# A DeltaNet scan with values scaled on GpSimd, decayed keys on ScalarE, another product order, and the gate's input split inside the scan

## The chip, the cores and the metric

The kernel runs on one core of one Trainium2 chip. The metric is the device time of one execution in microseconds (us), as a median of runs. It is one program with five engines that work through instruction lists of their own and wait for each other by semaphores: TensorE (PE, with its weight loads PEld), VectorE (DVE), ScalarE (ACT), GpSimd (POOL) and SyncE (SP), which issues the weight transfers.

## What is computed

Two blocks of a transformer on 256 latent and 256 context tokens of width 1024, in float32. The change touches only the second block, from the gated delta rule to the gate:

```python
def gated_delta_chunked(q, k, v, beta, g, s0):
    ...
    a = jnp.where(strict, jnp.einsum("bhnid,bhnjd->bhnij", kb, k) * decay, 0.0)
    t_inv = lax.linalg.triangular_solve(a + eye, ...)
    u = t_inv @ (v * beta[..., None])
    w = t_inv @ (kb * jnp.exp(g)[..., None])
    kd = k * jnp.exp(g_last[..., None] - g)[..., None]
    def step(s, inp):
        v_new = u_i - jnp.einsum("bhcd,bhde->bhce", w_i, s)
        o_i = (jnp.einsum("bhcd,bhde->bhce", qg_i, s)
               + jnp.einsum("bhij,bhje->bhie", attn_i, v_new))
        s = s * jnp.exp(gl_i)[..., None, None] + jnp.einsum("bhcd,bhce->bhde", kd_i, v_new)
        return s, o_i
...
gates = jax.nn.sigmoid((h @ w_gate + b_gate).astype(jnp.float32))   # 1024 -> 3072
```

It runs in two directions, over 4 chunks of 128 tokens (the kernel's own size) and 4 heads of 128.

## The kernel before

**Inverse by levels.** `level_step` (L1013) builds the inverse of four chunk matrices in 24 steps (`STEPS`), two groups of products a step. VectorE masks the first product (L2082), subtracts the second from `Y` (L2086) and masks the transposed root for the next level (L2071). GpSimd makes `YR` (L2275). The last four steps finish `Y` for chunks 0, 1, 2, 3 in that order.

**Scan.** `TT[d]` is `Y` under the triangular mask of direction d: eight masks (L2093), all on VectorE, after the last level step. Then come four steps s. `SCAN` gives the chunk of each: 2, 3, 0, 1 for direction 0 and 3, 2, 1, 0 for direction 1. Chunks 0 and 1 are the latent ones, so only steps 2 and 3 have an output. At each step and for both directions:

- VectorE scales the values by beta (L2108, into `Xb` at step 0 and `BV` after) and the keys by their decay (L2115, `KD`), in four instructions of 128x128 for the four heads;
- TensorE multiplies keys by the state (group `ks`) and queries by the state (`o1`), and VectorE makes X from `ks` and `BV` (L2123);
- TensorE makes the new values `vn` = `TT` times X, and ScalarE copies them out (L1256, called in the loop of L1505);
- TensorE makes the state's addition `S` from `KD` and `vn`, and the second half of the output, `o2`. VectorE updates the state (L2145, L2147) and adds both halves to the output (L2134, L2154).

A group is one PSUM bank. `heads` (L995) fills it with four products, at L998 as the profile shows them; a float32 product leaves two records in it. Groups take banks 0 to 4 in turn. After each of the first three steps stands one block of the conditioning matrix (`ada_block`, L607, 16 records), which also frees a slot of the three-slot weight ring, so that SyncE can issue a transfer of the gate's weights.

**Between scan and gate.** TensorE folds the conditioning (L618) and transposes the output (L1087). VectorE adds the bias (L1576) and copies the transposes out (L2162). The gate's input h is split in two parts so that products run in a faster number format: ScalarE rounds it to `gate_hi` (L1516) and VectorE takes the rest, `gate_lo` (L2165), in eight pieces. The weights are split the same way in parts of 128x1024, with room for three: `w_hi` by ScalarE (L1271), `w_lo` by VectorE (L1732). A part has 8 x 3 products (L550, L551, L552) and makes one of 24 gate groups. With `lead=True` the first three parts run interleaved. `keep_busy` (L480) issues filler products whose result is thrown away: 12 before the first `vn`, 14 and 2 at the gate (two records each).

## Time and profile before

| | us |
|---|---|
| median of three runs | 1786.26 |
| lowest, highest | 1779.35, 1787.01 |
| span of the profiled execution | 1778.1 |
| levels of the inverse | some 1318 to 1372 |
| scan, first `vn` to the transposes | 1378 to 1417 |
| first product of the gate | 1423.37 |

The page gives a span for the profiled execution, from its first to its last instruction, and no time of its own beside it; the times of the runs lie 1.3 to 8.9 us above it. All times of the rows are us from the start of that span. A row of the timeline merges neighbouring instructions of one kind: start, how long they last together, engine, line, count, and in brackets how long the engine was idle before and what ended that.

### The profile page before, as it was taken

Reading aid. Unit: us, or ns where it says so; the run is one execution under the profiler, and the core shown is the slowest. Engines: PE = TensorE matmul, PEld = TensorE weight load, DVE = VectorE, ACT = ScalarE, POOL = GpSimd, SP = SyncE. Lnnn points to the kernel's source line nnn. Section 1 sums busy time; section 2 is a strip of 40 time slices with the busy share of each in tenths; the row PEclk is TensorE's granted clock in tenths of the full one; section 3 lists DMA queues with packets and bytes.
Section 4 is the critical chain, followed back from the end, with each engine's and each line's share of the span. In section 5 each row is a group of like instructions: output and inputs, shape, how many; then the busy total and the mean of one; then the engine's idle time right before and its main releaser. Section 6 shows DMA issues by size and latency. Waiting matters only on the chain.

```text
span 1778.1 us, 26580 instructions
## 1 busy us (share of the span) xinstructions
PE 1704.4 (96%) x10450; PEld 1364.7 (77%) x10450; DVE 969.5 (55%) x1732; ACT 692.9 (39%) x1255; POOL 193.1 (11%) x210
## 2 busy tenths in 40 slices
PE   5999999999999999999999999899999999999997
PEld 2775457778888887454689999777689799989997
DVE  3454654643434344346736666775588855555454
ACT  3433564332323232234635444643310266344443
POOL 1012442100000001043000000100134000200000
PEclk9999999999999999999999999999999999999999
DMA  9225981222222224334043555133130334435342
GB/s 407 84 95 239 378 331 48 95 95 95 95 95 95 95 95 151 130 143 189 2 179 150 190 190 188 53 145 139 53 137 2 142 143 153 178 143 190 148 158 74
DMA packets 21323, 254.02 MB, mean 143 GB/s; under 512 B 2256, under 2 KB 4560, under 8 KB 5584
## 3 DMA queue, kind: packets, MB, share of 16 engines
q1 hardware_dynamic: 18144, 242.51, 35.5%
q10 hardware_dynamic: 3056, 9.82, 1.5%
q8 instruction: 84, 1.38, 0.3%
q14 instruction: 39, 0.32, 0.1%
HBM read 251.26 MB, written 1.05 MB: 142 GB/s over the span
## 4 chain that ended last, share of the span: by engine, by line
PE 83%; DVE 8%; ACT 4%; issue 2%; DMA 2%; POOL 1%; DVEq 0%; POOLq 0%; ACTq 0%; SPq 0%
PE bank L550 18%; PE bank L551 17%; PE bank L552 17%; PE bank L507 10%; PE bank L998 4%; PE bank L607 3%; PE bank L686 3%; PE bank L712 2%; DVE w_lo L1732 2%; PE bank L694 2%; DMA weights<-in_ada 2%; ACT w_hi L1271 1%; DVE root L1593 1%; PE bank L661 1%; POOL root L2229 1%
## 5 line engine op out<-in xcount | busy, mean ns | idle before, releaser
L1732 DVE TENSOR_TENSOR w_lo<-weights,w_hi 128x1024 fp32r<-128x1024 f32 (+2 forms) x286 | 331.9, 1169 | 109.0 <-ACT w_hi L1271 106.2
L1271 ACT ACTIVATE w_hi<-weights 128x1024 fp32r<-128x1024 f32 (+2 forms) x286 | 287.7, 1013 | 231.8 <-PE bank L552 227.4
L550 PE MATMUL bank<-h_hi,w_hi 128*128 128x256 f32 (+1 forms) x1024 | 338.8, 331 | 14.2 <-DVE w_lo L1732 7.9
L552 PE MATMUL bank<-h_hi,w_lo 128*128 128x256 f32 (+1 forms) x1024 | 335.1, 327 | 0.0
L551 PE MATMUL bank<-h_lo,w_hi 128*128 128x256 f32 (+1 forms) x960 | 311.0, 324 | 0.0
L550 PEld LDWEIGHTS bank<-h_hi,w_hi 128*128 128x128 f32 x1024 | 192.6, 188 | 41.2 <-issue 19.6
L552 PEld LDWEIGHTS bank<-h_hi,w_lo 128*128 128x128 f32 x1024 | 192.2, 188 | 19.0
L551 PEld LDWEIGHTS bank<-h_lo,w_hi 128*128 128x128 f32 x960 | 180.8, 188 | 15.2
L551 PE MATMUL bank<-mlp_hidden_lo,w_hi 128*128 128x512 f32 (+1 forms) x512 | 174.4, 341 | 0.0
L550 PE MATMUL bank<-mlp_hidden_hi,w_hi 128*128 128x512 f32 (+1 forms) x512 | 173.2, 338 | 0.6 <-DVE w_lo L1732 0.6
L552 PE MATMUL bank<-mlp_hidden_hi,w_lo 128*128 128x512 f32 (+1 forms) x512 | 172.7, 337 | 0.0
L507 PE MATMUL bank<-slab,weights 128*128 128x256 f32 (+2 forms) x656 | 163.6, 402 | 0.9 <-ACT slab L1210 0.2
L507 PEld LDWEIGHTS bank<-slab,weights 128*128 128x128 f32 (+1 forms) x656 | 120.6, 186 | 42.3 <-issue 19.7
L2229 POOL TENSOR_TENSOR root<-root,sq 128x512 f32<-128x512 f32 (+1 forms) x42 | 47.7, 1136 | 940.5 <-ACT sq L1197 937.6
L1794 DVE SCALAR_TENSOR_TENSOR x<-bank,mod,x 128x256 f32<-128x256 f32 x104 | 47.4, 481 | 171.1 <-PE bank L552 171.1
L550 PEld LDWEIGHTS bank<-mlp_hidden_hi,w_hi 128*128 128x128 f32 x512 | 96.5, 189 | 13.8 <-issue 1.1
L1780 DVE TENSOR_TENSOR slab<-bank,slab 128x512 f32<-128x512 f32 (+1 forms) x64 | 35.7, 558 | 130.3 <-ACT slab L1301 130.3
L552 PEld LDWEIGHTS bank<-mlp_hidden_hi,w_lo 128*128 128x128 f32 x512 | 96.1, 188 | 11.5
L551 PEld LDWEIGHTS bank<-mlp_hidden_lo,w_hi 128*128 128x128 f32 x512 | 96.1, 188 | 11.0
L1301 ACT ACTIVATE slab<-bank 128x512 f32<-128x512 f32 (+1 forms) x64 | 31.4, 490 | 153.9 <-PE bank L552 153.9
L998 PE MATMUL bank<-slab 128*128 128x128 f32 x656 | 81.1, 277 | 7.8 <-DVEq L2128 3.4
L607 PE MATMUL bank<-weights,cond 128*32 128x512 f32 x576 | 71.8, 617 | 17.1 <-DMA weights<-in_ada 17.1
(276 smaller groups left out, 2849.0 us busy)
## 6 DMA issues: line engine op xcount, KB each, us to landing
weights<-in_ada SPq DMA_DIRECT2D x36, 2048.0 KB, 9.6
weights<-in_mlp_up SPq DMA_DIRECT2D x16, 2048.0 KB, 8.2
weights<-in_mlp_down SPq DMA_DIRECT2D x16, 2048.0 KB, 8.2
weights<-in_ffn_in SPq DMA_DIRECT2D x11, 2048.0 KB, 7.9
weights<-in_in SPq DMA_DIRECT2D x8, 2048.0 KB, 8.0
weights<-in_gate SPq DMA_DIRECT2D x6, 2048.0 KB, 7.9
weights<-in_ffn_out SPq DMA_DIRECT2D x8, 1408.0 KB, 6.1
weights<-in_even_in SPq DMA_DIRECT2D x3, 2048.0 KB, 12.5
```

Of the source, the lines that this page charges most:

```text
L507: last = mm(b[rows, 0:width], lhsT(k), rhs(k), start=k == 0, stop=k == kc - 1)
L550: mm(b[:, 0:width], wh, hi(k), start=k == 0, stop=False)
L551: mm(b[:, 0:width], wh, lo(k), start=False, stop=False)
L552: return mm(b[:, 0:width], wl, hi(k), start=False, stop=k == kc - 1)
L607: ins = mm(banks[ADA_BANK][strip, :], cond[:, n // 2, k, window], w[:, k, :], start=at == 0 and k < 4, stop=at == ADA_SIZES[batch] - 1 and ...
L686: close(mm(b[:, 0:u["n"]], u["q"], u["k"], start=True, stop=True), t)
L998: ins = mm(b[:, hd * P:(hd + 1) * P], lhsT(hd), rhs(hd), start=True, stop=True)
L1271: A(split_part(w_hi, q), raw_part(q), ACT.Copy).then_inc(sem("w_hi_ready"), 1)
L1732: V.tensor_tensor(split_part(w_lo, q), raw_part(q), split_part(w_hi, q).bitcast(F32), ALU.subtract)\
L1780: V.tensor_tensor(relu[name][:, i % 3, 0:width], bank(tb)[:, 0:width], relu[name][:, i % 3, 0:width], ALU.mult).then_inc(free(tb), 1)
L1794: ins = V.scalar_tensor_tensor(out=x[:, i % 8, cols], in0=bank(t)[:, cols], scalar=mod[n][:, 40 + i % 8, s:s + 1], in1=x[:, i % 8, cols], ...
L2229: nc.gpsimd.tensor_tensor(sq_sum[:, 0:width], sq_sum[:, 0:width], sq[:, c % 2, 0:width], ALU.add)\
```

## The change

Four things are done:

1. Of the eight masks VectorE keeps two, those of step 0 (`TT[0]` chunk 2, `TT[1]` chunk 3), each right behind the subtraction that finishes its `Y`. GpSimd makes the other six, a pair for each later step.
2. GpSimd scales the values: for step 0 before the levels, into `VN` (whose place in `work` changes), for the later steps into `Xb`, where X is then formed in place. ScalarE scales the keys. It does step 0's during the last level step, the others after the state product before.
3. TensorE does both `ks` first, then for each direction `o1` and at once `vn`. The filler of the scan and of the gate is gone.
4. ScalarE rounds the gate's input after step 2's new values, and the first weight parts are split during step 3 and behind it. The gate's products follow the scan directly and part by part, not interleaved. The transposes of the output come after the third part, the fold after the fourth; VectorE's copies and bias follow.

The semaphores of the norms are joined in two (`norm_sq`, `norm_added`), with counts in place of names.

```diff
@@ -332,7 +332,7 @@
...
-        Xb, VN, KD, BV, S = ([work[:, (2 * n + d) * 512:(2 * n + d + 1) * 512] for d in range(2)] for n in range(5))
+        Xb, S, KD, VN = ([work[:, (n + d) * 512:(n + d + 1) * 512] for d in range(2)] for n in (0, 2, 4, 7))
...
+                def state_read(tag, d, rows):
+                    t = SCAN[d][s]
+                    heads((tag, d, s), lambda hd: rows[:, hd, t * P:(t + 1) * P], lambda hd: S[d][:, hs(hd)])
+
+                def new_values(d):
+                    t = SCAN[d][s]
+                    if s:
+                        pe.wait_ge(sem("X_ready"), 2 * (s - 1) + d + 1)
+                        pe.wait_ge(sem("TT_rest"), 2 * (s - 1) + d + 1)
+                    else:
+                        pe.wait_ge(sem("X0_ready"), d + 1)
+                        pe.wait_ge(sem("TT_ready"), d + 1)
+                    heads(("vn", d, s), lambda hd: TT[d][:, t, hs(hd)], lambda hd: (Xb if s else VN)[d][:, hs(hd)])
+
+                if s:
+                    for d in range(2):
+                        drained(pe, ("S", d, s - 1))
+                        state_read("ks", d, kT)
+                for d in range(2):
+                    if SCAN[d][s] < 2:
+                        state_read("o1", d, qT)
+                    new_values(d)
...
-                    n = 2 * s + d
-                    if s:
-                        drained(pe, ("S", d, s - 1))
-                        heads(("ks", d, s), lambda hd: kT[:, hd, t * P:(t + 1) * P], lambda hd: S[d][:, hs(hd)])
-                    if t < 2:
-                        heads(("o1", d, s), lambda hd: qT[:, hd, t * P:(t + 1) * P], lambda hd: S[d][:, hs(hd)])
-                for d in range(2):
-                    t = SCAN[d][s]
-                    n = 2 * s + d
-                    if n:
-                        pe.wait_ge(sem("X_ready"), n + 1)
-                    else:
-                        b = open_group(("vn", d, s))
-                        keep_busy(b, 12)
-                        pe.wait_ge(sem("TT_ready"), 8)
-                        pe.wait_ge(sem("X_ready"), n + 1)
-                    heads(("vn", d, s), lambda hd: TT[d][:, t, hs(hd)], lambda hd: Xb[d][:, hs(hd)], opened=n == 0)
...
-            ada_fold(4)
-            for t in range(2):
-                pe.wait_ge(sem("o_ready"), t + 1)
-                b = open_group(("oT", t))
-                for hd in range(DN_HEADS):
-                    ins = nc.tensor.transpose(b[:, hs(hd)], otok[:, t, hs(hd)], ident)
-                close(ins, ("oT", t))
+
+            def output_turned():
+                for t in range(2):
+                    pe.wait_ge(sem("o_ready"), t + 1)
+                    b = open_group(("oT", t))
+                    for hd in range(DN_HEADS):
+                        ins = nc.tensor.transpose(b[:, hs(hd)], otok[:, t, hs(hd)], ident)
+                    close(ins, ("oT", t))
+
             def gate_steps(m):
+                if m == 2:
+                    output_turned()
+                if m == 3:
+                    ada_fold(4)
...
             split_linear("gate", range(6), lambda k: gate_hi[:, k, :], lambda k: gate_lo[:, k, :], LAT,
                          lambda m: ("gate", m), lambda k, m: pe.wait_ge(sem("gate_in"), k + 1) if m == 0 else None,
-                         lead=True, after=gate_steps, idle=(14, 2))
+                         after=gate_steps)
...
                 copy_out(("kt", t), ktok[:, t, :])
+            def decayed_keys(d, s):
+
+                t = SCAN[d][s]
+                drained(act, ("kt", t))
+                if s:
+                    filled(act, ("S", d, s - 1))
+                for hd in range(DN_HEADS):
+                    ins = A(KD[d][:, hd * P:(hd + 1) * P], ktok[:, t, hd * P:(hd + 1) * P], ACT.Copy,
+                            scale=eKD[:, t, 4 * d + hd:4 * d + hd + 1])
+                ins.then_inc(sem("KD_ready"), 1)
+
+            act.wait_ge(sem("G_exp"), 3)
+            filled(act, ("u", STEPS - 1))
+            for d in range(2):
+                decayed_keys(d, 0)
+            gate_first = parts_before("in2")
             for s in range(4):
+                if s == 3:
+                    filled(act, ("S", 1, 2))
+                    split_until(gate_first + 1)
                 for d in range(2):
                     if s:
                         filled(act, ("o2" if SCAN[d][s - 1] < 2 else "S", d, s - 1))
                     else:
-                        act.wait_ge(sem("TT_ready"), 8)
                         filled(act, ("tt", STEPS - 1))
                     copy_out(("vn", d, s), VN[d])
+                if s < 2:
+                    for d in range(2):
+                        decayed_keys(d, s + 1)
...
+            filled(act, ("vn", 1, 3))
+            split_until(gate_first + PARTS)
             ada_copy(4)
-            filled(act, ("oT", 1))
...
+                    t, d = (n - 1) % 4, (n - 1) % 4 - 2
+                    if n > STEPS - 4 and d >= 0:
+                        drained(dve, ("tt", n - 1))
+                        V.tensor_tensor(by_head(TT[d][:, t, :]), by_head(Y[:, t, :]), spread(k2(f"until{d}")), ALU.mult)\
+                            .then_inc(sem("TT_ready"), 1)
...
-            for t in range(4):
-                drained(dve, ("tt", STEPS - 4 + t))
-                for d in range(2):
-                    V.tensor_tensor(by_head(TT[d][:, t, :]), by_head(Y[:, t, :]), spread(k2(f"until{d}")), ALU.mult)\
-                        .then_inc(sem("TT_ready"), 1)
+            def rest_of_gate(c):
+                dve.wait_ge(sem("gate_in_hi"), c + 1)
+                V.tensor_tensor(gate_lo[:, c, :], h[:, c, 0:LAT], gate_hi[:, c, :].bitcast(F32), ALU.subtract)\
+                    .then_inc(sem("gate_in"), 1)
+
...
-                    dst = Xb[d] if s == 0 else BV[d]
-                    for hd in range(DN_HEADS):
-                        ins = V.tensor_scalar(dst[:, hs(hd)], vtok[t][:, hd // 2, (hd % 2) * P:(hd % 2 + 1) * P],
-                                              col(beta, hd), None, ALU.mult)
-                    link(ins)
-                    if s == 0:
-                        V.engine_nop().then_inc(sem("X_ready"), 1)
-                    if s < 3:
-                        for hd in range(DN_HEADS):
-                            ins = V.tensor_scalar(KD[d][:, hs(hd)], ktok[:, t, hs(hd)], col(eKD, hd), None, ALU.mult)
-                        link(ins)
-                        V.engine_nop().then_inc(sem("KD_ready"), 1)
...
                         filled(dve, ("ks", d, s))
+                        dve.wait_ge(sem("BV_ready"), 2 * (s - 1) + d + 1)
                         for hd in range(DN_HEADS):
                             ins = V.scalar_tensor_tensor(out=Xb[d][:, hs(hd)], in0=bank(("ks", d, s))[:, hs(hd)],
-                                                         scalar=col(nbeG, hd), in1=BV[d][:, hs(hd)],
+                                                         scalar=col(nbeG, d, hd), in1=Xb[d][:, hs(hd)],
...
+                    if s == 3:
+                        split_until(split[0] + 1)
...
+                if s == 3:
+                    filled(dve, ("vn", 1, 3))
+                    for c in range(DC):
+                        rest_of_gate(c)
+                    filled(dve, ("o2", 1, 3))
+                    split_until(split[0] + 1)
...
-            ada_bias(4)
-            for t in range(2):
-                filled(dve, ("oT", t))
...
             for i in range(24):
                 split_until(PART_END[("gate", i)] + PARTS - 1)
+                if i == 3:
+                    for t in range(2):
+                        filled(dve, ("oT", t))
+                        V.tensor_copy(onT[:, :, t * P:(t + 1) * P], by_head(bank(("oT", t))[:, :]))\
+                            .then_inc(free(("oT", t)), 1)
+                if i == 4:
+                    ada_bias(4)
...
+            def scaled_values(dst, d, t, name):
+
+                for a in range(2):
+                    ins = nc.gpsimd.tensor_tensor(
+                        by_head(dst)[:, 2 * a:2 * a + 2, :], vtok[t][:, a, :].rearrange("p (h c) -> p h c", c=P),
+                        beta[:, t, 4 * d + 2 * a:4 * d + 2 * a + 2].unsqueeze(2).to_broadcast([P, 2, P]), ALU.mult)
+                ins.then_inc(sem(name), 1)
+
+            filled(pool, ("f1", 3))
+            pool.wait_ge(sem("gate_parts"), 3)
+            for d in range(2):
+                drained(pool, ("vt", SCAN[d][0]))
+                scaled_values(VN[d], d, SCAN[d][0], "X0_ready")
...
+            filled(pool, ("tt", STEPS - 3))
+            for s in range(1, 4):
+                for d in range(2):
+                    drained(pool, ("vt", SCAN[d][s]))
+                    if s > 1:
+                        filled(pool, ("vn", d, s - 1))
+                    scaled_values(Xb[d], d, SCAN[d][s], "BV_ready")
+                for d in range(2):
+                    t = SCAN[d][s]
+                    drained(pool, ("tt", STEPS - 4 + t))
+                    nc.gpsimd.tensor_tensor(by_head(TT[d][:, t, :]), by_head(Y[:, t, :]),
+                                            k2(f"until{d}").unsqueeze(1).to_broadcast([P, DN_HEADS, P]), ALU.mult)\
+                        .then_inc(sem("TT_rest"), 1)
```

VectorE, from the last level steps to the first state copy. L2082 and L2086 (now L2122 and L2126) belong to the levels, L2093 (L2131) is the mask, L2108 values, L2115 keys, L2145 (L2180) the state's copy; ISA rows only signal. Before:

```order
L2082 TENSOR_TENSOR slab<-bank,consts 128x512
L2086 TENSOR_TENSOR slab<-slab,bank 128x512 x2
L2093 TENSOR_TENSOR slab<-slab,consts 128x512 x8
L2108 TENSOR_SCALAR slab<-slab 128x128 x4
L2112 ISA
L2115 TENSOR_SCALAR slab<-slab 128x128 x4
L2117 ISA
```

Now:

```order
L2122 TENSOR_TENSOR slab<-bank,consts 128x512
L2126 TENSOR_TENSOR slab<-slab,bank 128x512
L2131 TENSOR_TENSOR slab<-slab,consts 128x512
L2126 TENSOR_TENSOR slab<-slab,bank 128x512
L2131 TENSOR_TENSOR slab<-slab,consts 128x512
L2180 COPY slab<-bank 128x128 x4
```

Two masks remain, one of them between the last two subtractions, and the scaled sets are gone.

TensorE, from the last level steps over the scan to the gate. L998 (now L1006) are the groups of `heads`, L483 the filler, L607 (L615) conditioning, L618 the fold, L1087 the transposes. Before:

```order
L998 MATMUL bank<-slab 128x128 x20
L483 MATMUL bank<-shared 128x256 x12
L998 MATMUL bank<-slab 128x128 x16
L607 MATMUL bank<-weights,cond 32x512 x8
L998 MATMUL bank<-slab 128x128 x24
L607 MATMUL bank<-weights,cond 32x512 x8
L998 MATMUL bank<-slab 128x128 x40
L607 MATMUL bank<-weights,cond 32x512 x8
L998 MATMUL bank<-slab 128x128 x32
L618 MATMUL bank<-shared,root 128x32 x4
L1087 MATMUL bank<-shared,slab 128x128 x8
L483 MATMUL bank<-shared 128x256 x14
```

Now:

```order
L1006 MATMUL bank<-slab 128x128 x36
L615 MATMUL bank<-weights,cond 32x512 x8
L1006 MATMUL bank<-slab 128x128 x24
L615 MATMUL bank<-weights,cond 32x512 x8
L1006 MATMUL bank<-slab 128x128 x40
L615 MATMUL bank<-weights,cond 32x512 x8
L1006 MATMUL bank<-slab 128x128 x32
L558 MATMUL bank<-gate_hi,w_hi 128x256
```

The same groups stand there (20 + 16 = 36), without the filler, and the gate's first product follows the scan's last one.

GpSimd, from the diagonal matrices ahead of the levels (L2263, now L2297) to the sums at the gate's end (L2280, now L2340). L2275 (L2322) is `YR`, L2304 half a set of scaled values, L2334 a mask. Before:

```order
L2263 TENSOR_TENSOR slab<-shared,slab 128x512 x8
L2275 TENSOR_TENSOR slab<-slab,consts 128x512 x24
L2280 TENSOR_TENSOR slab<-slab 128x256 x8
```

Now:

```order
L2297 TENSOR_TENSOR slab<-shared,slab 128x512 x8
L2304 TENSOR_TENSOR slab<-slab 128x256 x4
L2322 TENSOR_TENSOR slab<-slab,consts 128x512 x24
L2304 TENSOR_TENSOR slab<-slab 128x256 x4
L2334 TENSOR_TENSOR slab<-slab,consts 128x512 x2
L2304 TENSOR_TENSOR slab<-slab 128x256 x4
L2334 TENSOR_TENSOR slab<-slab,consts 128x512 x2
L2304 TENSOR_TENSOR slab<-slab 128x256 x4
L2334 TENSOR_TENSOR slab<-slab,consts 128x512 x2
L2340 TENSOR_TENSOR slab<-slab 128x256 x8
```

Sixteen halves and six masks came to GpSimd, in the order in which the steps use them.

## Rows read from the trace of the kernel before

**Rows 1.** The page: the span, and the busy time of TensorE.
```profile
span 1778.1 us, 26580 instructions
PE 1704.4 (96%) x10450; PEld 1364.7 (77%) x10450; DVE 969.5 (55%) x1732; ACT 692.9 (39%) x1255; POOL 193.1 (11%) x210
```

**Rows 2.** Windows: length, busy PE, PEld, DVE, ACT, POOL, granted clock, DMA share, GB/s.
```profile
1385.00:1396.00 11.00, 8.60 (x69) 6.62 (x70) 8.12 (x33) 1.19 (x2) 0.00 (x0) 1.00 0.52 192
...
1436.00:1560.00 124.00, 122.24 (x906) 117.22 (x905) 71.12 (x100) 64.59 (x94) 12.07 (x13) 1.00 0.44 168
```

**Rows 3.** Timeline of TensorE, scan and gate: start, length, line, count, idle time before.
```profile
1378.22 1.13 PE L998 MATMUL bank<-slab 128*128 128x128 f32 x8 [1.35 <-DVEq L2112]
...
1383.05 1.92 PE L607 MATMUL bank<-weights,cond 128*32 128x512 f32 x16
...
1389.34 4.23 PE L998 MATMUL bank<-slab 128*128 128x128 f32 x32 [2.38 <-DVEq L2128]
1393.50 1.92 PE L607 MATMUL bank<-weights,cond 128*32 128x512 f32 x16
...
1406.33 1.93 PE L607 MATMUL bank<-weights,cond 128*32 128x512 f32 x16
1408.19 7.53 PE L998 MATMUL bank<-slab 128*128 128x128 f32 x64
...
1417.51 6.21 PE L483 MATMUL bank<-shared 128*128 128x256 f32 x28
1423.37 0.47 PE L550 MATMUL bank<-gate_hi,w_hi 128*128 128x256 f32 x1
...
1434.46 0.36 PE L550 MATMUL bank<-gate_hi,w_hi 128*128 128x256 f32 x1 [0.55 <-ACT w_hi L1271]
...
1437.42 0.28 PE L550 MATMUL bank<-gate_hi,w_hi 128*128 128x256 f32 x1
```

**Rows 4.** Timeline of VectorE, the same stretch.
```profile
1371.72 0.69 DVE L2086 TENSOR_TENSOR slab<-slab,bank 128x512 f32<-128x512 f32 x1 [0.38 <-PE bank L998]
1372.33 4.90 DVE L2093 TENSOR_TENSOR slab<-slab,consts 128x512 f32<-128x512 f32 x8
...
1388.08 2.29 DVE L2123 SCALAR_TENSOR_TENSOR slab<-bank,slab 128x128 f32<-128x128 f32 x8
...
1418.54 2.77 DVE L2165 TENSOR_TENSOR gate_lo<-slab,gate_hi 128x256 fp32r<-128x256 f32 x8
1421.25 3.50 DVE L1732 TENSOR_TENSOR w_lo<-weights,w_hi 128x1024 fp32r<-128x1024 f32 x3
```

**Rows 5.** Timeline of ScalarE: four scaled 128x128 pieces, and a copy of new values.
```profile
1266.28 1.28 ACT L1492 ACTIVATE slab<-slab 128x128 f32<-128x128 f32 x4 [1.33 <-DVEq L2017]
...
1379.46 0.60 ACT L1256 ACTIVATE slab<-bank 128x512 f32<-128x512 f32 x1 [68.31 <-PE bank L998]
```

**Rows 6.** Groups of GpSimd by line and shape: count, busy us, mean ns.
```profile
L2275 POOL TENSOR_TENSOR slab<-slab,consts 128x512 f32<-128x512 f32 x24 | 30.5, 1270 | 39.2 <-DVE slab L2086 19.7 <-DVE slab L2065 17.2 <-PE bank L998 2.3
L2238 POOL TENSOR_TENSOR slab<-slab,stat 128x256 f32<-128x256 f32 x32 | 20.7, 647 | 42.0 <-DVE stat L1704 41.9
```

**Rows 7.** DMA issues of the gate's weights: KB each, median us to landing.
```profile
weights<-in_gate SPq DMA_DIRECT2D x6, 2048.0 KB, 7.9
```

**Rows 8.** Timelines of VectorE and GpSimd where both work, ahead of and in the levels.
```profile
1311.98 0.69 DVE L2065 TENSOR_TENSOR slab<-slab,shared 128x512 f32<-128x512 f32 x1
...
1313.30 1.26 DVE L2065 TENSOR_TENSOR slab<-slab,shared 128x512 f32<-128x512 f32 x1
...
1327.23 0.68 DVE L2071 TENSOR_TENSOR slab<-bank,consts 128x512 f32<-128x512 f32 x1
...
1312.75 1.27 POOL L2275 TENSOR_TENSOR slab<-slab,consts 128x512 f32<-128x512 f32 x1 [15.96 <-DVE slab L2065]
...
1327.39 1.27 POOL L2275 TENSOR_TENSOR slab<-slab,consts 128x512 f32<-128x512 f32 x1 [0.95 <-DVE slab L2086]
```

**Rows 9.** Windows after TensorE's last product, columns as in rows 2.
```profile
1771.00:1773.00 2.00, 0.00 (x0) 0.00 (x0) 1.97 (x5) 0.00 (x0) 0.00 (x0) 0.54 0.01 3
```

68 lines of the change are left out of this document (30 added, 38 removed).

## The prediction, written before the run

> **What bounds the kernel now.** I read the page first: TensorE is busy for 96% of the span [rows 1], so only a place where it waits, or works for nothing, can give time back. Next I read the busy time by stretch. The gate's products are TensorE's own: 122.24 of 124 us busy, all at a granted clock of 1.00 [rows 2]. The scan before them is not: TensorE is busy for 8.60 of 11 us between 1385 and 1396. So I read the scan engine by engine in order of time. TensorE's rows [rows 3] show a wait of 1.35 us before the first new-value product (1378.22), one of 2.38 us before that of step 1 (1389.34), and at 1417.51 a run of 28 filler records, 6.21 us of products on a constant that nobody reads (`keep_busy`), until the gate's first product at 1423.37. More such filler (24 records) stands ahead of 1378.22. VectorE's rows [rows 4] say what is waited for. From 1372.33 it applies eight masks, at 4.90/8 = 0.61 us each; then it scales values (L2108) and keys, four instructions of 128x128 a set, at every step; the 1.35 us end with the mark behind the first values (L2112) [rows 3]. Both stand in front of what TensorE needs next. After the scan come eight rests of the gate's input (2.77 us) and three rests of weights (3.50 us), all after the transposes of the output.
>
> **The units of the sum.** One product group (four heads) has 8 records. The 64 records from 1408.19 take 7.53 us; without the last one's tail, some 0.15 us, that is 0.92 us a group. The stretches with waits look like 0.95, and I take 0.95. From its start to the next start a conditioning block (16 records, L607) holds TensorE for 1.85 us (1.92 less the tail) [rows 3]. One part of the gate's weights is 24 products; from 1434.46 to 1437.42 that is 2.96 with a slow first one, 2.88 without (24 x 0.12). ScalarE copies new values in 0.60 us [rows 5]. For a hand-over between engines I take 0.13 us: the copy starts at 1379.46, 1.24 us after its product of 1.1 us.
>
> **Part 1, the masks (gain 6.0 us).** Before, the first new-value product starts at 1378.22, behind eight masks and the first values. Now VectorE applies one mask right behind the subtraction it belongs to. The subtraction before the last ends near 1371.4, since the last one starts at 1371.72 after an idle 0.38 us [rows 4]. So the first mask runs 1371.4 to 1372.1 and TensorE starts at 1372.2. This pushes the last subtraction from 1371.72 to 1372.1; it and the second mask end near 1373.5. The first values are ready long before, from GpSimd at about 1297. The last piece of the order above shows the six masks on GpSimd. A mask of that form costs it 1.27 us, and half a set of values I put at the nearest row, 0.65 us [rows 6], so a pair of sets is 2.6 and a pair of masks 2.5 us. They start at 1368.9 and are due at steps 1, 2 and 3. For step 2 GpSimd begins when the step 1 products are done (about 1382.2) and is finished by 1387.3, while TensorE wants the two masks from 1389.8. For step 3 it is finished by 1396.7 and wanted at 1401.1. The spare is at least 2.5 us, so I cost them at nothing; the cover is the state products, the conditioning block and the read-outs.
>
> **Part 2, steps 0 to 2 (gain 0.5 + 2.0 + 1.5 us).** First product to first conditioning block is 4.83 us before (1378.22 to 1383.05). Now the second product waits for the second mask (1.4 us after the first); with its copy and the two state products I get 4.4, say 0.5 less. From that block to the next is 10.45 us before (1383.05 to 1393.50). Now it is 1.85 + 6 x 0.95 = 7.55, plus 0.9 for X: VectorE's correction takes 1.14 us a set (2.29 for two at 1388.08 [rows 4]) and can't hide wholly behind one group. That makes 8.45, or 2.0 less. From there to the third block it is 12.83 us before (1393.50 to 1406.33) and now 1.85 + 10 x 0.95 = 11.35. The read-outs stand ahead of each new-value product and hide the correction, so 1.5 less. The decayed keys cost ScalarE 1.28 us a set by the nearest row [rows 5]; two sets (2.5 us) follow each state product, 5 us before TensorE wants them, in time in which ScalarE does nothing now.
>
> **Part 3, end of scan to the gate (gain 7.5 us).** Before, 1406.33 to 1423.37 is 17.04 us. Now TensorE has 1.85 + 8 x 0.95 = 9.45 us of work and then the gate's first product, with no fold, no transposes and no filler between. What must be ready then: one part of weights split on both engines (w_hi near 1397, w_lo 1402.7) and the first rest of the gate's input, which VectorE writes after two corrections, one w_lo and two read-outs, by my count at 1405.8. TensorE finishes at 1405.9. That is a near tie, so I add 0.1: 9.55, or 7.5 less. The rests then come every 0.35 us (2.77/8), and TensorE uses one in 0.36. The gate's first block has landed: its transfer is issued when the first conditioning block has used its slot, and takes 7.9 us [rows 7]; now that is near 1378.6, and the block is there by 1387. The next ones come behind blocks two and three, wanted at 1412 and 1424.
>
> **Part 4, the first gate parts (gain 0).** First to fourth part is 11.09 us before (1423.37 to 1434.46), with filler and a wait in it. Now three parts of 2.88, 0.6 us in which the second part's w_lo is late (VectorE comes to it only after eight rests), and 0.9 for the two transposes, moved here, make 10.1. The fold, another 0.95 (0.98 before the scan's end), moved behind the fourth part, makes 11.05. From there the stretch is TensorE's, as before. Copying the transposed output and the bias moved with them, into VectorE time that has room (71 of 124 us busy [rows 2]).
>
> **The sum.** 6.0 + 0.5 + 2.0 + 1.5 + 7.5 + 0 = 17.5 us less. The page's execution has a span of 1778.1 us [rows 1], which becomes 1760.6; the three times are 1.3, 8.2 and 8.9 us above that span. On the median it gives 1786.3 - 17.5 = 1768.8 us. With no wait in the scan at all (28 groups and 3 blocks, 32.15 us, against some 33.7 in my count) and none at the second part, the gain would be 19.7 us. With every near tie lost, 14 us.
>
> **A page against the trace: one lock for two engines.** The trace shows VectorE held by GpSimd in one kind of instruction: L2065, two inputs in SBUF, takes 0.69 us alone (1311.98), but 1.26 us when GpSimd's instruction of 1312.75 to 1314.02 is under way (1313.30) [rows 8]. L2071, which reads a bank and one SBUF tensor, keeps its 0.68 us (1327.23) beside a GpSimd instruction from 1327.39 on. The Trainium skill, page SBUF — State Buffer, section SBUF: two separate sides, says just this: the pair is an exclusive lock, kept for a whole instruction, against two-SBUF-input VectorE instructions. By that rule, moving work to GpSimd is a danger in itself. In the scan, however, nearly all of VectorE's work reads a bank. What is exposed is the two masks. The second is released together with GpSimd's first mask, by the same subtraction; if GpSimd takes the lock first, the second product comes up to 1.3 us later. At 1311.98 and 1312.75 VectorE went first (0.04 us against 0.08 after the release), so I leave it out of the sum and keep it for rival (a). By the skill's rule with GpSimd first the sum would be 16.2 us and the time 1770.1; with VectorE first it stands.
>
> **Rivals.**
> (a) *Ties lost.* The second mask is blocked (1.3 us), hand-overs cost 0.2 rather than 0.13 us (0.7), and gate_lo and the second part come 1 to 2 us later. The gain is then 9 to 14 us, 1772 to 1777. For it: three near ties. Against: each has a row.
> (b) *The gate gives it back.* Parts 1 to 3 are now split while VectorE also adds the last read-outs and copies the output. If the split ran a part late (2.9 us) for three parts, 8.7 us would be lost: gain 8.8, 1777.5. Against: a part costs VectorE 1.2 us of 2.88.
> (c) *GpSimd sets the scan.* From 2.5 us over, each further microsecond goes on the path. It needs masks and values at twice their rows, 10.2 us for 5.1: 2 x 2.6 us late, gain 12, 1774.
> (d) *Slower: the clock.* The filler keeps TensorE working; 28 products of it (56 records) go. After its last product at the end TensorE's granted clock falls to 0.54 within 1771 to 1773, that is toward 1.2 GHz [rows 9]. If that came at the scan's start and stayed, 32.15 us of work would take twice as long: 1786.3 - 17.5 + 32.2 = 1801. It decides from 17.5 us of work at 1.2 GHz. Against: TensorE works for 32.15 of 33.7 us in the new scan, more than in 1385 to 1396, where waits of up to 2.38 us left the clock at 1.00 [rows 2, 3].
> (e) *The change doesn't do what it says.* The new order excludes that: the masks, the filler and the scaled sets have left their places.
>
> **How the numbers follow.** Forecast (14 to 19.7 us less): 0.68. (a) 0.15. (b) and (c) together 0.10. (d) 0.04. 0.03 for a gain near zero by a cause I don't see. Predicted: 1768.8 us. The range takes the gain from 10.5 to 19.7 us and the spread of the times themselves (1779.4 to 1787.0): 1758 to 1776. A difference of over 0.5% (8.9 us) is about what a measurement of this kernel tells from none. Faster by that: all of the forecast, (a), and part of (b) and (c), 0.87. Within: 0.09. Slower: 0.04.
>
> **What would show it.** In the changed trace: the first new-value product 0.8 us behind the first mask; conditioning blocks 8.5 and 11.4 us apart (10.45 and 12.83 now); the gate's first product 9.5 us after the third block starts, with the gate_lo row touching it; six GpSimd masks of 1.3 us; a granted clock of 1.00 throughout. Wrong would be: the second mask at 1.2 us or more, TensorE waiting for GpSimd, or waits between the first gate parts above 1 us.

## The result, and the profile after

The changed kernel takes 1765.28 us (median of four runs, 1762.58 to 1766.02), the kernel before beside it 1784.9 us. The ratio is 0.9895 with a 95% interval of 0.988 to 0.991: 1.05% faster. In a second comparison it was 0.9889 (0.9871 to 0.9906).

The page after, beside [rows 1]: the span is 14.7 us shorter, TensorE's busy time 10.1 us.

```profile
span 1763.4 us, 26446 instructions
PE 1694.3 (96%) x10394; PEld 1356.3 (77%) x10394; DVE 953.5 (54%) x1670; ACT 700.5 (40%) x1279; POOL 210.4 (12%) x232
```

Windows of the changed kernel over scan and gate, columns as in [rows 2]. TensorE is busy for 29.25 of the 30 us from 1380 to 1410, where [rows 2] showed 8.60 of 11, and the granted clock stays at 1.00.

```profile
1380.00:1390.00 10.00, 9.51 (x80) 6.35 (x75) 5.35 (x20) 5.09 (x16) 4.46 (x6) 1.00 0.56 211
1390.00:1400.00 10.00, 10.00 (x92) 9.30 (x92) 7.55 (x26) 4.60 (x12) 5.21 (x7) 1.00 0.56 211
1400.00:1410.00 10.00, 9.74 (x88) 8.42 (x77) 7.73 (x23) 3.62 (x6) 0.00 (x0) 1.00 0.56 210
1410.00:1425.00 15.00, 14.62 (x123) 14.44 (x123) 11.06 (x15) 6.93 (x9) 0.00 (x0) 1.00 0.37 142
```

TensorE's timeline of the changed kernel, to be held against [rows 3]. L1006 are the groups of `heads`, L615 conditioning, L558 a gate product, L1098 the transposes, L626 the fold.

```profile
1375.57 1.13 PE L1006 MATMUL bank<-slab 128*128 128x128 f32 x8 [0.49 <-issue]
1376.90 3.03 PE L1006 MATMUL bank<-slab 128*128 128x128 f32 x24 [0.20 <-issue]
1379.86 1.93 PE L615 MATMUL bank<-weights,cond 128*32 128x512 f32 x16
...
1384.17 4.30 PE L1006 MATMUL bank<-slab 128*128 128x128 f32 x32 [0.40 <-DVEq L2155]
1388.41 1.92 PE L615 MATMUL bank<-weights,cond 128*32 128x512 f32 x16
1390.26 9.20 PE L1006 MATMUL bank<-slab 128*128 128x128 f32 x80
1399.39 1.92 PE L615 MATMUL bank<-weights,cond 128*32 128x512 f32 x16
1401.24 7.53 PE L1006 MATMUL bank<-slab 128*128 128x128 f32 x64
1409.04 0.36 PE L558 MATMUL bank<-gate_hi,w_hi 128*128 128x256 f32 x1 [0.26 <-DVE gate_lo L2137]
...
1412.52 0.36 PE L558 MATMUL bank<-gate_hi,w_hi 128*128 128x256 f32 x1 [0.38 <-DVE w_lo L1772]
...
1418.35 1.03 PE L1098 MATMUL bank<-shared,slab 128*128 128x128 f32 x8
1419.14 0.36 PE L558 MATMUL bank<-gate_hi,w_hi 128*128 128x256 f32 x1
1422.10 0.97 PE L626 MATMUL bank<-shared,root 128*128 128x32 f32 x8
1422.90 0.36 PE L558 MATMUL bank<-gate_hi,w_hi 128*128 128x256 f32 x1
```

No wait is above 0.49 us, and no filler stands between. Two rows run on without a gap: 80 records from 1390.26, 64 from 1401.24.

VectorE's timeline beside it, to be held against [rows 4]: L2126 is a level's subtraction, L2131 a mask, L2180 the state's copy, L2150 X, L1772 a rest of weights, L2163 the first half of the output, L2137 the rests of the gate's input.

```profile
1374.06 0.69 DVE L2126 TENSOR_TENSOR slab<-slab,bank 128x512 f32<-128x512 f32 x1 [0.20 <-PE bank L1006]
1374.78 0.69 DVE L2131 TENSOR_TENSOR slab<-slab,consts 128x512 f32<-128x512 f32 x1
1375.39 0.68 DVE L2126 TENSOR_TENSOR slab<-slab,bank 128x512 f32<-128x512 f32 x1
1376.11 0.69 DVE L2131 TENSOR_TENSOR slab<-slab,consts 128x512 f32<-128x512 f32 x1
1378.96 1.90 DVE L2180 COPY slab<-bank 128x128 f32<-128x128 f32 x8 [2.16 <-PE bank L1006]
...
1402.44 2.37 DVE L2150 SCALAR_TENSOR_TENSOR slab<-bank,slab 128x128 f32<-128x128 f32 x8 [1.89 <-PE bank L1006]
1404.92 1.23 DVE L1772 TENSOR_TENSOR w_lo<-weights,w_hi 128x1024 fp32r<-128x1024 f32 x1
1406.07 2.28 DVE L2163 SCALAR_TENSOR_TENSOR slab<-bank,slab 128x128 f32<-128x128 f32 x8
1408.46 2.77 DVE L2137 TENSOR_TENSOR gate_lo<-slab,gate_hi 128x256 fp32r<-128x256 f32 x8
```

**A measure that the rest of the kernel doesn't blur.** I cut every span in three: the *arrival*, up to the start of VectorE's last-but-one subtraction; the *landmark*, from there to the start of the gate's fifth part (1437.42 in [rows 3], 1422.90 after); and what follows. The arrival lies ahead of the scan. That subtraction in VectorE's timeline of the kernel before:

```profile
1370.66 0.69 DVE L2086 TENSOR_TENSOR slab<-slab,bank 128x512 f32<-128x512 f32 x1 [0.20 <-PE bank L998]
```

| kernel | median us | ratio (95%) | arrival | landmark | what follows |
|---|---|---|---|---|---|
| before | 1784.9 | | 1370.66 | 66.76 | 340.68 |
| after | 1765.28 | 0.9895 (0.988 to 0.991) | 1374.06 | 48.84 | 340.50 |
| after, again | 1764.77 | 0.9889 (0.9871 to 0.9906) | 1373.72 | 48.84 | 340.44 |
| e1 before, no filler | 1786.76 | 1.0011 (1.0002 to 1.002) | 1373.41 | 70.26 | 340.63 |
| e2 masks behind | 1762.87 | 0.9882 (0.9865 to 0.9898) | 1370.42 | 48.84 | 340.44 |
| e3 masks ahead | 1773.13 | 0.993 (0.991 to 0.9951) | 1375.21 | 56.04 | 340.55 |
| e4 sets on VectorE | 1772.49 | 0.994 (0.9921 to 0.9959) | 1372.48 | 57.34 | 340.48 |
| e5 gate late | 1770.39 | 0.9917 (0.9895 to 0.9939) | 1374.46 | 55.41 | 340.43 |
| e6 old order | 1764.6 | 0.9896 (0.9873 to 0.9918) | 1370.83 | 49.50 | 340.57 |
| e7 GpSimd busy | 1765.01, one run | | 1372.96 | 49.79 | 340.45 |
| e8 rest early | 1763.95 | 0.9884 (0.9867 to 0.99) | 1375.32 | 47.74 | 340.54 |
| e9 filler back | 1769.03 | 0.9914 (0.9899 to 0.9929) | 1373.21 | 52.86 | 340.53 |
| e10 both | 1763.4 | 0.9882 (0.9867 to 0.9898) | 1373.38 | 47.74 | 340.58 |

The last column is the same within 0.25 us in all thirteen. The whole effect sits in the landmark: 66.76 - 48.84 = 17.92 us. The arrival scatters over 4.9 us. In these two traces it is 3.40 us later in the changed kernel, which leaves 17.92 + 0.18 - 3.40 = 14.7 us between the spans. Most of that scatter is TensorE's clock, not the change. I took windows of 10 us up to 1370 and added up TensorE's busy time times what the granted clock lacks to 1.00. The loss is 2.9 us before and 6.0 after; it is 5.7 in e1, whose code up to there is that of before and whose arrival is 2.75 us later. Over all thirteen traces it runs from 1.7 (e2, the earliest arrival) to 6.2 us (e8, the latest), and a line through loss and arrival has a slope of 1.0, with every trace within some 0.8 us of it.

### The profile page after: what moved, and what is told of

It reads as the page before. It is cut to its first block, busy times and chain, and to the rows that moved or that the text cites. A ratio compares the mean times of both kernels' runs of the same rounds, so it can differ in the third digit from the quotient of the medians.

```text
span 1763.4 us, 26446 instructions
## 1 busy us (share of the span) xinstructions
PE 1694.3 (96%) x10394; PEld 1356.3 (77%) x10394; DVE 953.5 (54%) x1670; ACT 700.5 (40%) x1279; POOL 210.4 (12%) x232
## 3 DMA queue, kind: packets, MB, share of 16 engines
HBM read 251.26 MB, written 1.05 MB: 143 GB/s over the span
## 4 chain that ended last, share of the span: by engine, by line
PE 83%; DVE 7%; ACT 4%; issue 2%; DMA 2%; POOL 1%; DVEq 0%; POOLq 0%; ACTq 0%; SPq 0%
PE bank L558 18%; PE bank L560 17%; PE bank L559 17%; PE bank L515 11%; PE bank L1006 4%; PE bank L615 3%; PE bank L694 3%; PE bank L720 2%; DVE w_lo L1772 2%; PE bank L702 2%; DMA weights<-in_ada 2%; ACT w_hi L1287 1%; DVE root L1633 1%; PE bank L669 1%; POOL root L2263 1%
## 5 line engine op out<-in xcount | busy, mean ns | idle before, releaser
L1772 DVE TENSOR_TENSOR w_lo<-weights,w_hi 128x1024 fp32r<-128x1024 f32 (+2 forms) x286 | 331.9, 1169 | 103.4 <-ACT w_hi L1287 100.5
L558 PE MATMUL bank<-h_hi,w_hi 128*128 128x256 f32 (+1 forms) x1024 | 341.0, 333 | 14.2 <-DVE w_lo L1772 7.8
L558 PEld LDWEIGHTS bank<-h_hi,w_hi 128*128 128x128 f32 x1024 | 193.2, 189 | 40.1 <-issue 19.5
L558 PE MATMUL bank<-mlp_hidden_hi,w_hi 128*128 128x512 f32 (+1 forms) x512 | 174.9, 342 | 0.7 <-DVE w_lo L1772 0.7
L2263 POOL TENSOR_TENSOR root<-root,sq 128x512 f32<-128x512 f32 (+1 forms) x42 | 47.6, 1134 | 940.2 <-ACT sq L1213 937.4
L515 PEld LDWEIGHTS bank<-slab,weights 128*128 128x128 f32 (+1 forms) x656 | 120.6, 186 | 42.3 <-issue 19.7
L558 PEld LDWEIGHTS bank<-mlp_hidden_hi,w_hi 128*128 128x128 f32 x512 | 96.1, 188 | 12.4 <-issue 1.2
L615 PE MATMUL bank<-weights,cond 128*32 128x512 f32 x576 | 71.0, 611 | 17.5 <-DMA weights<-in_ada 17.5
L1341 ACT ACTIVATE slab<-bank,stat 128x512 f32<-128x512 f32 (+1 forms) x96 | 59.2, 617 | 62.9 <-DVE stat L1730 39.7
```

What stands on the lines that cost most here:

```text
L515: last = mm(b[rows, 0:width], lhsT(k), rhs(k), start=k == 0, stop=k == kc - 1)
L558: mm(b[:, 0:width], wh, hi(k), start=k == 0, stop=False)
L615: ins = mm(banks[ADA_BANK][strip, :], cond[:, n // 2, k, window], w[:, k, :], start=at == 0 and k < 4, stop=at == ADA_SIZES[batch] - 1 and ...
L1341: A(a["prob"][i % nprob][:, 0:u["n"]], bank(t)[:, 0:u["n"]], ACT.Exp, bias=stat[:, 1, i:i + 1], scale=a["scale"], accum_out=stat[:, 2, i:i ...
L1772: V.tensor_tensor(split_part(w_lo, q), raw_part(q), split_part(w_hi, q).bitcast(F32), ALU.subtract)\
L2263: nc.gpsimd.tensor_tensor(sq_sum[:, cols], sq_sum[:, cols], sq[:, c % 2, cols], ALU.add)\
```

## The experiments

**e1: is the filler dead weight?** The kernel before, without its filler products.

```diff
-                        keep_busy(b, 12)
...
-                         lead=True, after=gate_steps, idle=(14, 2))
+                         lead=True, after=gate_steps)
```

> The kernel before, with the filler of the scan (12 products) and of the gate (14 and 2) taken out and nothing else changed. Landmark: from the last level subtraction but one to the fifth gate part is 66.76 us before (1370.66 to 1437.42) and 48.84 us after the change (1374.06 to 1422.90). Theory A, the filler only fills waits for VectorE: 66 to 67 us, the first new-value product still 7.5 us after the landmark's start, granted clock 1.00 in the scan, time within 1 us of before. Theory B, the filler also holds the clock over TensorE's waits of some 6.5 us (before the first product) and 5 us (before the gate): the granted clock falls to 0.5 there, products at 1.2 GHz for some us, 3 to 10 us more than before.

TensorE's timeline and two windows of e1:

```profile
1380.97 6.29 PE L998 MATMUL bank<-slab 128*128 128x128 f32 x32 [6.53 <-DVEq L2111]
...
1426.89 0.55 PE L550 MATMUL bank<-gate_hi,w_hi 128*128 128x256 f32 x1 [5.05 <-DVE w_lo L1731]
...
1380.00:1390.00 10.00, 9.03 (x56) 7.44 (x57) 6.69 (x32) 1.19 (x2) 0.00 (x0) 0.70 0.01 2
...
1430.00:1440.00 10.00, 9.29 (x64) 9.09 (x62) 0.65 (x1) 2.10 (x4) 0.00 (x0) 0.81 0.00 0
```

The first product comes no sooner (7.56 us behind the subtraction, as before). Now TensorE stands idle for 6.53 us, and then works at a lower granted clock: the first four groups take 6.29 us. First product to first block is 6.22 us against 4.83. At the gate the wait is 5.05 us, the products run 0.21 us apart up to 1433.67 and 0.12 after, and first to fifth part is 16.78 us against 14.05. Only one thing comes back: third block to gate is 16.39 us against 17.04, so the gate's filler had outlasted its wait by 0.65 us. The landmark is 3.5 us longer, which is theory B at its lower end; the median time is 2.25 us longer, with an interval that just clears 1. The filler gained more where it stood than it cost.

**e9: and in the changed kernel?** The filler put back.

```diff
+                        if d == 0:
+                            keep_busy(open_group(("vn", d, s)), 12)
...
-                         after=gate_steps)
+                         after=gate_steps, idle=(14, 2))
```

> The changed kernel with TensorE's filler products put back: 12 ahead of the first new values, and 14 and 7 times 2 in the gate's first parts, as the kernel before has them. In the changed kernel TensorE waits 0.49 us ahead of the first new values and at most 0.4 us at any place in the gate's first parts. Theory A (the filler now has no wait to stand in, so it costs its own length): 12 products of 0.22 us minus 0.49 us is 2.2 us, and 28 products 6.2 us minus 0.6 us of waits is 5.6 us; landmark 48.84 + 7.8 = about 56.6 us, ratio about 0.993 to 0.994. Rival B (the filler is free, since it only stands while splits are awaited): landmark 49 to 50.

```profile
1374.08 5.34 PE L491 MATMUL bank<-shared 128*128 128x256 f32 x24
1379.26 2.96 PE L1006 MATMUL bank<-slab 128*128 128x128 f32 x24
```

My edit and my count were both partly wrong. `idle` acts only with `lead=True`, which the change gave up, so none stood at the gate. And a filler product leaves two records of 0.22 us, so twelve last 5.34 us. The first product then comes 6.05 us behind the subtraction instead of 1.51, and the landmark is 4.0 us longer. So theory A holds in kind, not in size: filler of 5.34 us without a wait of that length costs 4.0 us, and most of what comes off is the short waits of step 0, 0.49 us ahead of the first product and 0.51 us behind it. The filler at the gate was not tried.

**e3: all eight masks ahead again**, on VectorE, with the rest of the change kept.

```diff
-                        pe.wait_ge(sem("TT_ready"), d + 1)
+                        pe.wait_ge(sem("TT_ready"), 8)
...
+            for t in range(4):
+                drained(dve, ("tt", STEPS - 4 + t))
+                for d in range(2):
+                    V.tensor_tensor(by_head(TT[d][:, t, :]), by_head(Y[:, t, :]), spread(k2(f"until{d}")), ALU.mult)\
+                        .then_inc(sem("TT_ready"), 1)
...
```

> The changed kernel with all eight masks on VectorE behind the last subtraction and every new-value product waiting for all of them, as in the kernel before; everything else as changed. My sum: the first product comes 8 x 0.61 us and a hand-over behind the last subtraction, 6.4 us after the last but one in place of 1.51: landmark 53.6 us, 4.8 more than the changed kernel. Rival, part of that is given back because TensorE otherwise waits later in steps 0 and 1 (0.2 and 0.4 us): 53.0 us.

TensorE's timeline, and a window, of e3:

```profile
1381.88 6.40 PE L1006 MATMUL bank<-slab 128*128 128x128 f32 x32 [5.64 <-issue]
...
1380.00:1390.00 10.00, 8.12 (x48) 6.66 (x48) 3.55 (x11) 3.64 (x10) 0.00 (x0) 0.66 0.01 2
```

The first product is 5.16 us later, and after the 5.64 us of idleness four groups take 6.40 us: first product to first block is 6.34 us against 4.29. Together 7.2 us, of which the 2.05 behind the first product are the clock (0.66 in the window). My sum of 4.8 and the rival's 4.2 had no term for it; ahead of the first product my sum is near (5.16 us).

**e2: masks on VectorE, but behind.** The six masks of steps 1 to 3 on VectorE, after the two of step 0; GpSimd makes only the values.

```diff
+            for s in range(1, 4):
+                for d in range(2):
...
+                    V.tensor_tensor(by_head(TT[d][:, t, :]), by_head(Y[:, t, :]), spread(k2(f"until{d}")), ALU.mult)\
...
-                    nc.gpsimd.tensor_tensor(by_head(TT[d][:, t, :]), by_head(Y[:, t, :]),
...
```

> The changed kernel with the six later masks back on VectorE, directly behind the two of step 0; GpSimd keeps the values only. Theory A, only the two masks ahead of the first product matter, since VectorE waits 2.16 us for the first state product and TensorE has the conditioning block behind it: first state copy 1.5 us later, first product unchanged, landmark 48.8 to 49.8 us (48.84 in the changed kernel). Rival, moving the masks off VectorE is what gives the gain: 6 x 0.61 = 3.7 us on the path, landmark 52.5 us.

The landmark is 48.84 us, to the last digit that of the change. VectorE's six masks take 3.69 us; its first copy of the state comes 1.4 us later for them (6.27 us behind the last-but-one subtraction, not 4.90), and TensorE has the conditioning block to do meanwhile. What the masks gain is by which of them stand ahead of the first product, not by GpSimd.

**e4: the scaled sets on VectorE again**, steps 1 to 3.

```diff
...
+                        for hd in range(DN_HEADS):
+                            ins = V.tensor_scalar(Xb[d][:, hs(hd)], vtok[t][:, hd // 2, (hd % 2) * P:(hd % 2 + 1) * P],
+                                                  col(beta, d, hd), None, ALU.mult)
...
+                        if s < 3:
+                            for hd in range(DN_HEADS):
+                                ins = V.tensor_scalar(KD[d][:, hs(hd)], ktok[:, t, hs(hd)], col(eKD, d, hd), None, ALU.mult)
...
-                        dve.wait_ge(sem("BV_ready"), 2 * (s - 1) + d + 1)
```

> The changed kernel, but VectorE again makes the values times beta and the decayed keys of steps 1 to 3, ahead of each step's own values; the masks stay where the change puts them. Landmark: from the start of VectorE's last-but-one level subtraction to the start of the gate's fifth part, 48.84 us in the changed kernel, 66.76 in the kernel before. Theory A (the sets cost what VectorE spends between a state's last copy and the next product): each of steps 1 and 2 gets some 1.5 us longer, step 3, which has no keys, little; landmark 51.5 to 53, ratio to the kernel before about 0.991. Rival B (the sets fit into VectorE's idle time ahead of the step's own values): landmark 49 to 50, ratio as the changed kernel's, 0.989 to 0.990.

TensorE, VectorE and GpSimd in e4's timelines, and a window:

```profile
1386.97 6.16 PE L1006 MATMUL bank<-slab 128*128 128x128 f32 x32 [4.78 <-DVEq L2167]
...
1379.84 2.93 DVE L2151 TENSOR_SCALAR slab<-slab 128x128 f32<-128x128 f32 x4 [0.57 <-DVEq L2198]
...
1383.89 0.88 DVE L2151 TENSOR_SCALAR slab<-slab 128x128 f32<-128x128 f32 x4 [0.21 <-DVE slab L2156]
...
1374.63 7.85 POOL L2341 TENSOR_TENSOR slab<-slab,consts 128x512 f32<-128x512 f32 x6 [6.35 <-DVE slab L2123]
...
1387.00:1393.00 6.00, 6.00 (x32) 5.94 (x32) 1.73 (x7) 1.19 (x2) 0.00 (x0) 0.59 0.01 5
```

Both theories were too low: the landmark is 57.34 us, 8.5 more than after. Step 1 alone is 6.23 us longer (14.78 against 8.55). The scaled sets put 4.4 us of wait on the path (4.78 against 0.40): their own instructions, and 2.05 us in which VectorE's first four stand still beside GpSimd's masks (2.93 us where the next four take 0.88, until the last mask ends at 1382.48). The two fit together: before, with the same sets and no such stand-still, the wait was 2.38 us [rows 3]. Then the clock is down again (0.59 in 1387 to 1393, four groups in 6.16 us, not 4.30). Step 2 is 2.26 us longer, step 3 not at all.

**e5: the gate's input split after the transposes**, as before the change, with fold and transposes ahead of the gate and no filler.

```diff
...
-                if s == 3:
-                    filled(dve, ("vn", 1, 3))
-                    for c in range(DC):
-                        rest_of_gate(c)
...
+            for c in range(DC):
+                rest_of_gate(c)
```

> The changed kernel with the gate's input and the first weight parts split after the transposes of the output, fold and transposes ahead of the gate as before; no filler, parts one by one. Theory A (my sum of part 3): fold, transposes, copy, eight rests and one w_lo stand between the last scan product and the gate's first: that distance is some 6.8 us in place of 0.3, of which 1.6 us come back because fold and transposes no longer stand among the parts: landmark 53.6 us, 4.8 more. Rival B, TensorE's wait of 4 to 5 us also lowers the granted clock: 2 to 4 us more on top, with a clock below 1.00 in the first gate parts.

TensorE's timeline, and a window, of e5:

```profile
1416.19 0.55 PE L558 MATMUL bank<-gate_hi,w_hi 128*128 128x256 f32 x1 [5.06 <-DVE w_lo L1763]
...
1416.20:1420.80 4.60, 4.60 (x21) 4.60 (x22) 2.00 (x2) 1.65 (x2) 0.00 (x0) 0.50 0.00 0
```

Third block to gate is 16.40 us against 9.65, first to fifth part 13.68 against 13.86, although fold and transposes no longer lie between: the products run 0.21 us apart up to 1420.80, at a granted clock of 0.50, and 0.12 after. The landmark is 6.6 us longer, 55.4 against theory A's 53.6. The wait is real, and the clock comes on top, with 1.8 us a little less than rival B's 2 to 4.

**e6: the old order of products.** Each direction's `o1` right behind its `ks`, then both `vn`; the rest is the changed kernel.

```diff
-                if s:
-                    for d in range(2):
+                for d in range(2):
+                    if s:
                         drained(pe, ("S", d, s - 1))
                         state_read("ks", d, kT)
-                for d in range(2):
                     if SCAN[d][s] < 2:
                         state_read("o1", d, qT)
+                for d in range(2):
                     new_values(d)
```

> The changed kernel with the older order of TensorE's products in a step: reads of the state for both directions with their outputs between, then both new values (in the changed kernel: both key reads, then output and new values of direction 0, then of direction 1). Theory A (VectorE's own values of direction 0 take 1.2 us after the key reads, which in the new order are covered by the first output's 1.0 us, in the old order by both): the old order frees the key reads' second half 0.5 us later in the steps with an output ahead of it, and gains it back; landmark 48.4 to 49.6. Rival B (the order carries part of the gain): landmark 50 or more, with TensorE waits of 0.5 us or more at the new values of steps 1 to 3.

TensorE's timeline of e6, in step 3:

```profile
1404.82 2.02 PE L1006 MATMUL bank<-slab 128*128 128x128 f32 x16 [1.06 <-DVEq L2167]
```

The landmark is 49.50, 0.66 us longer, in the range of A; but the wait of 1.06 us is there too, at `o2` in step 3 and not at the new values. L2167 is the mark behind VectorE's first output half, which comes later because the two sets of X now come 0.66 us apart. The order is worth 0.66 us of the landmark here: 0.12 in step 2, 0.67 in step 3, less 0.13 that comes back in the gate's first parts.

**e7: GpSimd busy when the masks come due.** One more product of two SBUF tensors on GpSimd, whose result is unused.

```diff
+                if s == 1:
+                    nc.gpsimd.tensor_tensor(sq[:, 0, :], ktok[:, 0, :], ktok[:, 1, :], ALU.mult)
```

> The changed kernel with one more product on GpSimd, 128x512 of two inputs in SBUF, right behind the four operations of its first values of step 1, so that it runs while VectorE's two masks come due; its output is read by nobody. Theory A (the two engines take turns at SBUF when both have two such inputs, as one row of the kernel before showed, 1.26 us instead of 0.69): VectorE's first mask takes 1.2 to 2.4 us instead of 0.69 and the first new values start up to 2 us after the last-but-one level subtraction's 1.51; landmark up to 50.5. Rival B (no such turns): the mask keeps its 0.69 us, the landmark its 48.84.

VectorE's mask and GpSimd's product in e7's timelines:

```profile
1373.69 1.63 DVE L2131 TENSOR_TENSOR slab<-slab,consts 128x512 f32<-128x512 f32 x1
...
1373.51 1.26 POOL L2332 TENSOR_TENSOR sq<-slab 128x512 f32<-128x512 f32 x1
```

GpSimd had started first, and the mask ends 0.55 us after GpSimd does: 1.63 us instead of 0.69. The landmark is 0.95 us longer, all of it this mask. Theory A holds, at its lower end.

**e8 and e10: one step further.** In e8 VectorE takes the gate's first rest of weights ahead of step 3's X, in its 1.89 us of idle time, and not behind it. e10 is e8 with e2's masks.

```diff
                 if s:
+                    if s == 3:
+                        split_until(split[0] + 1)
                     for d in range(2):
...
-                    if s == 3:
-                        split_until(split[0] + 1)
```

> The changed kernel with one step moved: VectorE takes the rest of the gate's first weight part ahead of its values of step 3, in the 1.89 us in which it waits for the key reads there, instead of behind them, so that it is 1.23 us earlier done with all that stands behind. Theory A (the waits of 0.26, 0.38 and 0.3 us of TensorE at the gate's first products hang on that chain): landmark 48.2 to 48.4 and 0.5 us of the time, 1764.5. Rival B (the waits come from ScalarE's splits or the weight transfer): landmark 48.8, nothing gained. Rival C (the step is late by its weight part, and the values of step 3 behind it too): landmark above 49.

> The move of the run beside it, and the six masks of steps 1 to 3 on VectorE again, behind the two of step 0, so that GpSimd makes the values alone and the two engines never hold SBUF against each other in the scan. Theory A (the masks are free on either engine, the move gives 0.5 us): landmark 48.2 to 48.4, 1764.5 us, and no GpSimd operation above 1.3 us. Rival B (the masks on VectorE, 3.7 us, push its later work until the moved step comes too late): landmark above 49.

> The changed kernel again, beside the two that follow: 1765 us by every theory, 1762 to 1768 by the spread of its first runs.

VectorE and TensorE in e8's timelines:

```profile
1401.92 1.23 DVE L1772 TENSOR_TENSOR w_lo<-weights,w_hi 128x1024 fp32r<-128x1024 f32 x1
1403.70 2.37 DVE L2152 SCALAR_TENSOR_TENSOR slab<-bank,slab 128x128 f32<-128x128 f32 x8 [0.55 <-PE bank L1006]
...
1402.50 7.53 PE L1006 MATMUL bank<-slab 128*128 128x128 f32 x64
1409.79 0.37 PE L558 MATMUL bank<-gate_hi,w_hi 128*128 128x256 f32 x1
```

The waits ahead of the gate's first product and its second part are gone, and the landmark is 47.74 us in both, 1.1 us less than after, twice what I expected: the gap ahead of the first product was 0.5 us wide (64 records to gate 7.80 us, now 7.29), and first product to transposes shrank from 9.31 to 8.72. The medians (1763.95 and 1763.4, against 1764.77 for after on the same chip) lie the same way, but their intervals overlap: the gain is read from the landmark, not from the times. That e10's landmark is e8's shows again that the masks are free on either engine; GpSimd's sets keep their length there (2.32 and 2.43 us for two).

## Why the prediction was right, step by step

| step | forecast | measured |
|---|---|---|
| part 1: subtraction to first product | 6.0 less | 7.56 to 1.51: 6.05 less |
| part 2: first product to block 1 | 0.5 less | 4.83 to 4.29: 0.54 less |
| block 1 to 2 | 8.45 | 8.55 |
| block 2 to 3 | 11.35 | 10.98 |
| part 3: block 3 to gate | 9.55 | 9.65 |
| part 4: first to fourth part | 10.1 | 10.10 |
| sum, to the fifth part | 17.5 less | 17.92 less |

**The mechanism.** Each interval is within 0.4 us of its forecast. The largest miss, block 2 to 3, is a term I priced too high: ten groups take 9.13 us to the next block's start, 0.91 each, where I took 0.95, a figure read from stretches with waits although I added waits apart. In two intervals this error hides another one. From block 1 to 2 the exposed part of X is 1.2 us (8.55 - 1.86 - 6 x 0.91), not 0.9. From block 3 to the gate the near tie is 0.51 us, as e8 shows by removing it (the profile marks 0.26 of it as idle), where I put 0.1; block and groups take 9.14 us, not 9.45. So the agreement to 0.1 us in these two is partly luck. GpSimd's spare, 2.5 us by my count, was about 2.6 for its masks of step 2: its masks for step 2 end at 1390.37, and the first `vn` there starts near 1390.26 + 3 x 0.91 = 1393.

**The time.** 1768.8 was forecast and 1765.28 came. Of the 3.5 us, 0.4 are the sum. 1.4 us are the base: I subtracted from the median of three runs, 1786.26, while the medians of before in four comparisons were 1784.9, 1784.51, 1783.96 and 1783.73. From 1784.9 and the measured 17.92 us follows 1767.0; the last 1.7 us stay open. They are not chance alone: in each of the eleven comparisons the medians lie 0.7 to 3.7 us more in favour of the run than its landmark does, in e1 too (2.25 us lost by the median, 3.5 by the landmark). The one trace of before is of a quick execution. Wherever a run's time and span are both known, the time is 1.8 to 1.9 us the longer, so 1778.1 belongs to a time near 1779.9, 5 us below the median, while 1763.4 belongs to the changed kernel's 1765.17. So the usual execution of before loses more than its trace shows. Over the whole span most executions of before have a lower granted clock (1784.5 to 1786.5 us at 0.993, 1779.1 and 1779.9 us at 0.997), so the clock is the likely cause, but none of the slower ones was traced. The forecast for the page's own execution, 1760.6, missed in the other direction (1763.4), by the arrival. Two bounds of the prediction don't follow from its own terms: 1779.4 - 19.7 is 1759.7, not 1758, and rival (a) adds up to 4 to 6 us lost, a gain of 11.5 to 13.5, with no term behind its 9. Neither decides anything here.

**Rival (a), the lock.** In the changed kernel VectorE had the mask first. Its second mask kept 0.69 us (1376.11), and GpSimd's first was the one to wait; its timeline shows two masks in 3.00 us at step 1 and in 2.51 at step 2:

```profile
1376.15 3.00 POOL L2334 TENSOR_TENSOR slab<-slab,consts 128x512 f32<-128x512 f32 x2 [1.51 <-DVE slab L2126]
...
1387.86 2.51 POOL L2334 TENSOR_TENSOR slab<-slab,consts 128x512 f32<-128x512 f32 x2
```

So leaving it out of the sum came out right. It was a bet on the order of two starts 0.04 us apart, and e7 shows that the danger was real: 0.95 us once GpSimd is first. e4 widens it. I had written that what is exposed is two inputs in SBUF, but L2151 in e4 reads only one SBUF tensor and waited too (1.30 us for the longest, 0.28 for most). The Trainium skill, page SBUF — State Buffer, section SBUF: two separate sides, names both kinds, VectorE instructions in a two-port mode and those with two SBUF inputs; I had used half of the sentence. e4 fits it, though no row here tells the mode of L2151.

**Rivals (b) and (c)** didn't come: the longest wait between the first gate parts is 0.38 us, and TensorE waits for GpSimd nowhere in the scan.

**Rival (d), the clock,** had the right cause and the wrong price. The granted clock stayed at 1.00 in the scan, where no wait is above 0.49 us; waits of up to 2.38 us had left it there before. But in e1, e3, e4 and e5 TensorE idled for 4.8 to 6.5 us without filler, and each time the products behind ran at 1.2 GHz. I had priced that as 32 us of work at half speed. It costs 1.4 to 2.7 us a time, because the clock comes back while TensorE works: in e3 it is 0.66 in 1380 to 1390 and 1.00 in the next window.

**What the prediction didn't see** is what its own sum rests on. It counted the filler as work that can go. e1 shows that by itself its removal loses 3.5 us. It can go only because the waits it stood in went with it. And because the parts protect one another, what they lose when undone one at a time is not what they gained: e3 (7.2), e4 (8.5) and e5 (6.6) lose 22.3 us together, where the whole change gained 17.9. Some 6 us of what they lose is the clock (2.05, 1.86 and, for 21 products 0.22 instead of 0.12 us apart, 2.1), which the kernel before, with its filler, does not pay; 2.05 us more are e4's stand-still beside GpSimd, which it doesn't pay either. That leaves some 14.2 us. The first values, which e3 leaves off the path (its first product comes 6.67 us behind the subtraction, not 7.56), make 0.89, the gate filler's overrun 0.65 (e1) and the order of products 0.66 (e6). That is 16.4 of 17.9 us; the last 1.5 are tied to no single part.

## What to carry to other kernels

Look for what an engine does ahead of the instruction that the bottleneck waits for, and leave there only what it reads: here two masks of eight. Take filler that stands in a wait out together with the wait: alone it lost 3.5 us here, and kept without its wait it cost 4.0. Compare landmarks inside the trace before spans: in the two traces of the changed kernel the landmark is the same to 0.01 us, while its start scatters by five over the runs.
